# A two-layer transformer block with a hybrid mixer, then a second block with experts: another order of the last third of the mixer stage

## The chip, the cores and the metric

The kernel is one program on one core of a Trainium2 chip. The metric is the device time of one execution in microseconds; three executions of the kernel before gave 3403.52, 3405.39 and 3412.49 us, with the median at 3405.39 us.

## What is computed

The reference runs two layers of a first block (feed-forward, hybrid mixer, feed-forward, each added to the residual stream x) on 512 tokens of width 1024, and then a second block that the change does not touch. The change is in the hybrid mixer, which the kernel runs twice. The reference, cut to it:

```python
def hybrid_mixer(h, layer_idx, w_in, w_out, ...):
    proj = h @ w_in
    mq, mk, mv, mo, mi, mf, z, xbc, dt_raw, dq, dk, dv = jnp.split(proj, split_idx, axis=-1)
    ...
    hm = mlstm_chunkwise(...)                                   # 4 heads of 64
    y_mlstm = jax.nn.sigmoid(mo) * rms_norm(hm, mlstm_norm_w)
    ...
    y = (ssd_chunked(xs, dt, A, Bm, Cm) + D_skip * xs) * jax.nn.silu(z)
    y_ssm = rms_norm(y.reshape(..., SSM_GROUPS, -1), ssm_norm_w)  # 2 groups of 256
    dq, dk = rms_norm(dq, q_norm_w), rms_norm(dk, k_norm_w)
    o = diff_attention(dq, dk, dv, rel_bias, lam)               # 4 heads, causal, blocks of 128 queries
    y_diff = rms_norm(o, subln_w) * (1.0 - lam_init)
    return jnp.concatenate([y_mlstm, y_ssm, y_diff], axis=-1) @ w_out

def probs(qi, ki):                                              # inside a block of 128 queries
    logits = einsum(qi, ki) * scale + bias
    return softmax(where(mask, logits, -inf))
a = probs(q1, k1) - lam * probs(q2, k2)
out = einsum(a, v)
```

## The kernel before

The program is a list of stages. In each stage every engine walks the same list of steps, which `steps()` writes out by hand, and does its own part of each step; counting semaphores order the engines among each other, and each engine's own queue is strictly in the order of the steps. So the order in which `Mixer.steps()` yields decides what stands behind what on each engine.

**Items and sums.** The weights of the projections come as items, two halves of a block of 256 output columns. Items 0 to 17 of a mixer belong to earlier work. Items 18 and 19 give the attention's values (`dv`), 20 to 23 the gate z of the SSM, 24 and 25 the gate `mo` of the mLSTM; items 26 to 33 are the output projection. Every matrix product is made as three matmuls of a high and a low part (`mm3`). For a token item, `tok_pe` makes two tiles of 128 tokens of 24 matmuls each (128x256): 48 matmuls on TensorE, which then ticks `("sum", i)`. An item of the output projection is 24 matmuls of 128x512 (`fm_pe`), over eight 128-wide chunks of y in the order 2, 3, 4, 5 (SSM), 0, 1 (mLSTM), 6, 7 (attention).

**Splitting.** Before item i, `ahead(i)` yields `split` of item i+2: ScalarE casts the weights to the high part (`split_act`, line 387), GpSimd subtracts it to get the low part (`split_lo`, a line 167 operation on POOL). There are three buffers in turn, so the cast waits until the sum that reads the buffer has ended: for an even item i that is sum i-1, for an odd item i it is sum i itself. A token sum with an even number needs the low part of the item after it.

**Attention tiles.** The differential attention has 16 tiles, four heads times four blocks of queries. Tile n has width w = 128, 256, 384 or 512 (n mod 4). The step `diff` n is a software pipeline. On TensorE (`diff_pe`): the product with the values of tile n-3 (128x64), the two logit products qk of tile n (32x128 by w, into banks 2 and 3), the transposes of tile n-2. On VectorE (`diff_dve`): for tile n-1 a reciprocal (line 1894), a small product, a scaling and the difference of the two softmaxes; for tile n the two biased logits L (line 177, out of PSUM), two maxima (line 1914) and their negation `neg`. On ScalarE (`diff_act`): two copies out of PSUM for tiles n-3 (line 1875) and n-2 (line 1880), and the two exponentials of tile n (line 182). So a tile goes round a loop of VectorE and ScalarE: reciprocal and difference of the tile before, L, maxima, `neg`, exponentials, next reciprocal.

**What stands around them.** `droot` and `dfin` finish the norm of the attention's q and k: a reciprocal on VectorE, a root on ScalarE, and then `dfin`, 64 matmuls of 32x128 and four products on VectorE. `mnorm` 0 to 8 is the mLSTM norm (0 to 3 squares on POOL, 4 a reduction on VectorE, then four scalings), `zgate` and `ssq` the gate and the sums of squares of the SSM output, `sroot` and `snorm` its norm, `dnorm` the norm of the attention's output, `mo` the mLSTM gate. `turn` c transposes chunk c of y (4 transposes on TensorE), ScalarE casts the high part (line 2048) and VectorE subtracts the low part; then chunk c is ready for the output sums.

**Order before.** Items 18 and 19; `mnorm` 0 to 4, `droot`, `dfin`; then for each of items 20 to 25 the whole sum and behind it three attention steps; then `sroot`, `snorm` 0, turns 2 and 3, the last attention step, `snorm` 1, turns 4 and 5, `mo`, turns 0 and 1, `dnorm` 5 to 8, turns 6 and 7, and the eight output sums.

## Time and profile before

| | |
|---|---|
| median of three executions | 3405.39 us (3403.52 to 3412.49) |
| the profiled execution | 3405.64 us |
| its span, first to last instruction | 3403.4 us |
| mean granted TensorE clock | 0.947 |
| TensorE matmul busy | 3124.8 us (92%) |
| VectorE / ScalarE / GpSimd busy | 1641.5 / 1040.0 / 237.3 us |
| HBM traffic | 129 GB/s over the span |

"Busy" is the union of an engine's instructions; the granted clock is a share of full speed, 1.0 or 0.5 at any moment, and a mean over a stretch otherwise. The profiled execution is 0.25 us above the median.

### The profile page before, as it was taken

Reading aid. Unit: us, or ns where it says so; the run is one execution under the profiler, and the core shown is the slowest. Engines: PE = TensorE matmul, PEld = TensorE weight load, DVE = VectorE, ACT = ScalarE, POOL = GpSimd, SP = SyncE. Lnnn points to the kernel's source line nnn. Section 1 sums busy time; section 2 is a strip of 40 time slices with the busy share of each in tenths; the row PEclk is TensorE's granted clock in tenths of the full one; section 3 lists DMA queues with packets and bytes.
Section 4 is the critical chain, followed back from the end, with each engine's and each line's share of the span. In section 5 each row is a group of like instructions: output and inputs, shape, how many; then the busy total and the mean of one; then the engine's idle time right before and its main releaser. Section 6 shows DMA issues by size and latency. Waiting matters only on the chain. (4 is left out here: it accounts for less than half of the span.)

```text
span 3403.4 us, 41878 instructions
## 1 busy us (share of the span) xinstructions
PE 3124.8 (92%) x17296; PEld 2377.4 (70%) x17296; DVE 1641.5 (48%) x3102; ACT 1040.0 (31%) x2121; POOL 237.3 (7%) x171
## 2 busy tenths in 40 slices
PE   8999989879999999999999769999898899787887
PEld 6777768757888878888788658888686888332333
DVE  5444474364555554555563555444643674311212
ACT  4222245243323243333344333222332553000002
POOL 0000032121000000000121220000000210000000
PEclk9999989779999999999998779999889899899999
DMA  5443421102223222212211102222212004899997
GB/s 191 179 163 147 150 73 50 38 25 75 99 87 115 84 93 86 70 69 81 87 62 38 38 25 87 93 102 90 78 62 75 2 2 174 328 421 421 421 421 308
DMA packets 66164, 443.36 MB, mean 130 GB/s; under 512 B 7476, under 2 KB 7732, under 8 KB 19640
## 3 DMA queue, kind: packets, MB, share of 16 engines
q1 hardware_dynamic: 61056, 423.65, 32.8%
q10 hardware_dynamic: 3224, 10.49, 0.8%
q0 software_dynamic: 1696, 6.55, 0.5%
q8 instruction: 137, 2.24, 0.3%
q14 instruction: 51, 0.42, 0.0%
HBM read 435.16 MB, written 5.51 MB: 129 GB/s over the span
## 5 line engine op out<-in xcount | busy, mean ns | idle before, releaser
L157 PE MATMUL ps<-b,b 128*128 128x512 f32 (+7 forms) x13982 | 2799.8, 394 | 175.8 <-DVE b L167 58.4
L157 PEld LDWEIGHTS ps<-b,b 128*128 128x128 f32 (+3 forms) x13982 | 2097.1, 184 | 846.2 <-issue 321.3
L167 DVE TENSOR_TENSOR b<-b,b 128x1024 fp32r<-128x1024 f32 (+9 forms) x734 | 598.5, 820 | 274.1 <-ACT b L387 162.4
L387 ACT CAST b<-b 128x1024 fp32r<-128x1024 f32 (+2 forms) x408 | 392.0, 962 | 442.7 <-PE ps L157 437.5
L167 DVE TENSOR_TENSOR b<-ps,b 128x64 f32<-128x64 f32 (+5 forms) x617 | 215.3, 363 | 329.4 <-PE ps L157 274.2
L157 PE MATMUL ps<-b 64*64 64x64 f32 (+10 forms) x2848 | 268.0, 283 | 43.8 <-ACT b L1880 26.2
L167 POOL TENSOR_TENSOR b<-b,b 128x1024 fp32r<-128x1024 f32 (+3 forms) x120 | 202.8, 1706 | 1377.6 <-ACT b L387 947.2
L157 PEld LDWEIGHTS ps<-b 64*64 64x64 f32 (+3 forms) x2848 | 224.4, 164 | 83.5 <-ACT b L1880 31.2
L177 DVE SCALAR_TENSOR_TENSOR b<-ps,b 128x512 f32<-128x512 f32 (+3 forms) x272 | 142.4, 545 | 236.3 <-PE ps L157 211.7
L183 ACT ACTIVATE b<-b 128x512 f32<-128x512 f32 (+8 forms) x294 | 156.1, 538 | 236.1 <-DVE b L177 192.7
L167 DVE TENSOR_TENSOR b<-b,ps 128x512 f32<-128x512 f32 (+1 forms) x106 | 71.8, 678 | 280.0 <-PE ps L157 271.6
L177 DVE SCALAR_TENSOR_TENSOR b<-ps,b,b 128x128 f32<-128x128 f32 (+3 forms) x172 | 89.2, 545 | 222.4 <-ACT b L183 126.6
L1453 ACT CAST b<-b 128x512 fp32r<-128x512 f32 x88 | 54.6, 621 | 409.8 <-DVE b L167 409.8
L177 DVE SCALAR_TENSOR_TENSOR b<-b,b,b 128x512 f32<-128x512 f32 (+3 forms) x204 | 155.9, 778 | 43.2 <-ACT b L183 38.8
L183 ACT ACTIVATE b<-ps 128x512 f32<-128x512 f32 (+5 forms) x114 | 48.4, 439 | 382.3 <-PE ps L157 381.1
L177 DVE SCALAR_TENSOR_TENSOR b<-b,b 128x512 f32<-128x512 f32 (+6 forms) x235 | 142.9, 622 | 40.7 <-ACT b L183 38.2
L183 ACT ACTIVATE b<-b,b 128x128 f32<-128x128 f32 (+2 forms) x240 | 102.0, 465 | 121.1 <-DVE b L167 106.7
L285 PE MATMUL ps<-b,b 128*128 128x128 f32 (+2 forms) x466 | 85.5, 326 | 51.4 <-DVE b L177 30.0
L285 PEld LDWEIGHTS ps<-b,b 128*128 128x128 f32 (+2 forms) x466 | 62.2, 165 | 88.5 <-DVE b L177 33.5
L183 ACT ACTIVATE b<-ps,b 128x128 f32<-128x128 f32 (+3 forms) x148 | 59.9, 442 | 132.6 <-PE ps L157 129.7
L1018 ACT COPY b<-ps 128x128 f32<-128x128 f32 x240 | 60.2, 269 | 79.1 <-PE ps L157 69.6
L1133 POOL MEMSET b<- 128x128 f32 x12 | 2.6, 265 | 1010.0 <-DVE b L2545 586.9
(99 smaller groups left out, 559.6 us busy)
## 6 DMA issues: line engine op xcount, KB each, us to landing
b<-in_eg SPq DMA_DIRECT2D x64, 1024.0 KB, 27.3
b<-in_eu SPq DMA_DIRECT2D x64, 1024.0 KB, 27.2
b<-in_ed SPq DMA_DIRECT2D x64, 1024.0 KB, 27.1
b<-in_wg SPq DMA_DIRECT2D x44, 1024.0 KB, 4.8
b<-in_wu SPq DMA_DIRECT2D x44, 1024.0 KB, 4.9
b<-in_win SPq DMA_DIRECT2D x40, 1024.0 KB, 4.8
b<-in_wd SPq DMA_DIRECT2D x48, 768.0 KB, 4.2
b<-in_wmod SPq DMA_DIRECT2D x24, 1024.0 KB, 5.3
```

The source lines that it names most:

```text
L157: return e.h.matmul(out, l, r, start=start, stop=stop)
L167: return e.h.tensor_tensor(out, a, b, op)
L177: return e.h.scalar_tensor_tensor(out, a, s, b, op0, op1)
L183: return e.h.activation(out, a, f, bias=bias, scale=scale)
L285: return e.h.transpose(out, i, self.K["ident"][0:n, 0:n])
L387: e.h.copy(hi, src).then_inc(*self.S.tick(("hi", i)))
L1018: e.h.copy(self.LB[q][:, 0:128], B[:, 0:128]).then_inc(*S.tick((s, j, "L", lev + 1)))
L1133: z = e.h.memset(t, 0.0)
L1453: e.h.copy(self.ahi[:, f - self.f0[grp], :], t).then_inc(*S.tick(("ahi", f)))
```

## The change

In `Mixer.steps()`:

- `droot` comes ahead of `mnorm` 0 to 4, the second root is a step of its own (`mroot`), and `dfin` stands behind the whole sum of item 20 instead of ahead of it, followed by attention steps 0 and 1.
- Items 21 to 25 are cut in two on TensorE: `suma` i makes the first token tile (24 matmuls), then comes one attention step, then `sum` i makes the second tile and ticks. Two attention steps follow for items 21 to 24, none for item 25.
- Attention steps 15 to 18 stand in the tail, with `sroot`, `snorm` 0, turns 2, 3 behind step 15, `snorm` 1, turns 4, 5 behind step 16, `mo`, two squares of `dnorm` and turns 0, 1 behind step 17.
- The first two output sums are begun early: `part` 0 (18 matmuls, chunks 2, 3, 4, 5, 0, 1) ahead of step 18, `part` 1 behind it. Their last six matmuls each wait for turns 6 and 7. The banks of the output sums go 4, 5, 6, 7 instead of 6, 7, 4, 5.

```diff
-        for t in (2 * half, 2 * half + 1):
+        for t in [2 * half + j for j in tiles]:
...
-        p.then_inc(*self.P.tick(("sum", i)))
+        if tiles[-1]:
+            p.then_inc(*self.P.tick(("sum", i)))
...
+    def out_pe(self, e, j, places):
+
+        i = self.np + j
+        hi, lo, _ = self.views(i)
+        e.wait_ge(self.lo.at(("lo", i)))
+        for n in places:
+            c = self.order[n]
+            e.wait_ge(self.V.at(("ylo", c)))
+            p = mm3(e, self.k.bank[self.bank(i)][:, :], (hi[:, c, :], lo[:, c, :]), self.op(c), n == 0, n == 7)
+        if places[-1] == 7:
+            p.then_inc(*self.P.tick(("sum", i)))
...
             yield from self.ahead(i)
+            if i > 20:
+                yield "suma", i
+                yield "diff", diff
+                diff += 1
             yield "sum", i
...
             if i == 19:
+                yield "droot", 0
                 for j in range(5):
                     yield "mnorm", j
-                yield "droot", 0
+                yield "mroot", 0
+            elif i == 20:
                 for j in (0, 2, 1, 3):
                     yield "dfin", j
-            if i >= 20:
-                for j in range(3):
+                yield "diff", 0
+                yield "diff", 1
+                diff = 2
+            elif i > 20:
+                n = 0 if i == 25 else 2
+                for j in range(n):
                     yield "diff", diff
                     diff += 1
-                    if j == 1 and i in (21, 22, 23, 24):
-                        yield "mnorm", i - 16
-                    if diff >= 16:
-                        yield "dnorm", diff - 16
+                if i < 25:
+                    yield "mnorm", i - 16
...
+        for n in range(diff, 19):
+            yield "diff", n
+            if n == 15:
+                yield "sroot", 0
+                yield "snorm", 0
+                yield "turn", 2
+                yield "turn", 3
+            elif n == 16:
+                yield "snorm", 1
+                yield "turn", 4
+                yield "turn", 5
+            elif n == 17:
+                yield "mo", 0
+                yield "dnorm", 0
+                yield "dnorm", 1
+                yield "turn", 0
+                yield "turn", 1
+                yield "part", 0
+            elif n == 18:
+                yield "part", 1
...
-            return (6, 7, 4, 5)[(i - self.np) % 4]
+            return 4 + (i - self.np) % 4
...
-                self.fm_pe(e, i, B[self.bank(i)], 512, self.op, lambda c: V.at(("ylo", c)), self.order)
+                self.out_pe(e, j, range(6, 8) if j < 2 else range(8))
```

On TensorE, around item 20 of the first mixer, the order changes like this (the 32x128 matmuls are `dfin`; 128x256 are those of a token sum; `b_126` 128x128, 128x256 and 128x384 are the qk products of tiles 0, 1 and 2; the row of line 285 is a transpose):

```order
@@ -2282,5 +2282,4 @@
 L157 MATMUL ps<-b_129,b_134 128x256
 L157 MATMUL ps<-b_54,b_72 128x4 x4
-L157 MATMUL ps<-b_54,b_117 32x128 x64
 L157 MATMUL ps<-b_127,b_133 128x256
 L157 MATMUL ps<-b_130,b_133 128x256
@@ -2331,8 +2330,7 @@
 L157 MATMUL ps<-b_131,b_133 128x256
 L157 MATMUL ps<-b_128,b_134 128x256
+L157 MATMUL ps<-b_54,b_117 32x128 x64
 L157 MATMUL ps<-b_126 128x128 x2
 L157 MATMUL ps<-b_126 128x256 x2
-L157 MATMUL ps<-b_126 128x384 x2
-L285 MATMUL ps<-b_54,b_126 128x128
```

The 64 matmuls of `dfin` move behind the 48 of sum 20, and the products of tile 2 move away from those of tile 1, behind the first half of sum 21.

On ScalarE, from the exponentials of tile 1 to those of tile 2 (line 182 with widths 256 and 384; line 387 is the cast of a weight split, here of item 23; line 1880, in the changed kernel 1912, is the copy of tile 0's transposes; the ACTIVATE of line 183 puts sum 21 away), before:

```order
L182 ACTIVATE b_126,b_121<-b_126,b_121 128x256
L1880 COPY b_126<-ps 128x128 [waits mix_sums]
L182 ACTIVATE b_126,b_122<-b_126,b_122 128x384 [waits mix_vecs]
L182 ACTIVATE b_126,b_122<-b_126,b_122 128x384
L387 CAST b_127<-b_51 128x1024 [waits mix_sums]
L183 ACTIVATE b_126<-ps 128x2x256
```

and now:

```order
L182 ACTIVATE b_126,b_121<-b_126,b_121 128x256
L387 CAST b_127<-b_51 128x1024 [waits mix_sums]
L1912 COPY b_126<-ps 128x128
L182 ACTIVATE b_126,b_122<-b_126,b_122 128x384 [waits mix_vecs]
L182 ACTIVATE b_126,b_122<-b_126,b_122 128x384
L183 ACTIVATE b_126<-ps 128x2x256
```

The cast, which waits for the whole of sum 21, now stands ahead of the exponentials of tile 2; the same holds at items 23 and 25 for tiles 8 and 14.

On TensorE in the tail (128x64 are products with the values; line 285 are transposes, those of the attention tiles and of the turns):

```order
 L157 MATMUL ps<-b_126 128x512 x2
-L285 MATMUL ps<-b_54,b_126 128x128 x2
+L285 MATMUL ps<-b_54,b_126 128x128 x10
 L157 MATMUL ps<-b_126 128x64 x2
-L285 MATMUL ps<-b_54,b_126 128x128 x3
+L285 MATMUL ps<-b_54,b_126 128x128 x11
 L157 MATMUL ps<-b_126 128x64 x3
 L285 MATMUL ps<-b_54,b_126 128x128 x12
-L157 MATMUL ps<-b_126 128x64 x4
-L285 MATMUL ps<-b_54,b_126 128x128 x24
 L157 MATMUL ps<-b_135,b_127 128x512
```

Eight transposes of turns follow each of tiles 15, 16 and 17's steps, and the product with the values of tile 15 (the x4) leaves its place ahead of the output sums; it now stands between the two part sums.

## Rows read from the trace of the kernel before

**Rows 1.** Windows, both mixers: stretch, us, busy PE PEld DVE ACT POOL, clock, DMA, GB/s

```profile
626.70:821.70 195.00, 150.73 (x901) 126.05 (x902) 101.49 (x223) 69.60 (x169) 42.02 (x25) 0.79 0.11 38
1869.20:2064.20 195.00, 149.56 (x901) 125.27 (x902) 99.95 (x224) 69.69 (x169) 42.01 (x25) 0.79 0.11 38
```

**Rows 2.** Windows of the first mixer, piece by piece

```profile
643.14:649.50 6.36, 6.36 (x129) 5.75 (x129) 2.24 (x3) 0.99 (x2) 2.36 (x1) 0.57 0.01 3
649.50:655.20 5.70, 5.70 (x50) 5.64 (x48) 0.75 (x1) 0.00 (x0) 0.00 (x0) 1.00 0.02 4
750.00:775.60 25.60, 9.15 (x41) 8.17 (x41) 13.90 (x31) 7.09 (x19) 0.75 (x1) 0.50 0.00 0
```

**Rows 3.** Timeline around `dfin`: start, us, engine, instruction, idle before and its releaser

```profile
636.02 2.34 POOL L167 TENSOR_TENSOR b<-b,b 128x1024 fp32r<-128x1024 f32 x1 [13.62 <-ACT b L387]
640.67 1.22 DVE L2214 TENSOR_REDUCE b<-b 128x16 f32<-128x1024 f32 x1 [4.81 <-POOL b L167]
643.14 12.21 PE L157 MATMUL ps<-b,b 128*32 128x128 f32 x176 [7.50 <-ACT b L183]
```

**Rows 4.** Timeline, reciprocals of tiles 0 to 4, 6, 7, 15

```profile
658.21 0.17 DVE L1894 RECIPROCAL b<-b 128x2 f32<-128x2 f32 x1 [1.33 <-ACT b L182]
661.95 0.17 DVE L1894 RECIPROCAL b<-b 128x2 f32<-128x2 f32 x1 [1.16 <-ACT b L182]
666.65 0.17 DVE L1894 RECIPROCAL b<-b 128x2 f32<-128x2 f32 x1 [1.37 <-ACT b L182]
674.97 0.17 DVE L1894 RECIPROCAL b<-b 128x2 f32<-128x2 f32 x1 [1.59 <-ACT b L182]
678.57 0.17 DVE L1894 RECIPROCAL b<-b 128x2 f32<-128x2 f32 x1 [0.17 <-ACT b L182]
691.82 0.17 DVE L1894 RECIPROCAL b<-b 128x2 f32<-128x2 f32 x1 [1.37 <-ACT b L182]
697.46 0.17 DVE L1894 RECIPROCAL b<-b 128x2 f32<-128x2 f32 x1 [0.80 <-ACT b L182]
746.28 0.17 DVE L1894 RECIPROCAL b<-b 128x2 f32<-128x2 f32 x1 [1.59 <-ACT b L182]
```

**Rows 5.** Timeline, logits and `neg` of tile 2, one undisturbed turn

```profile
663.14 1.01 DVE L177 SCALAR_TENSOR_TENSOR b<-ps,b 128x384 f32<-128x384 f32 x2
665.11 0.17 DVE L172 TENSOR_SCALAR b<-b 128x2 f32<-128x2 f32 x1
```

**Rows 6.** Timeline, token sum 21, and logits that waited for sums 21 and 22

```profile
661.70 7.75 PE L157 MATMUL ps<-b,b 128*128 128x256 f32 x48
670.70 1.29 DVE L177 SCALAR_TENSOR_TENSOR b<-ps,b 128x512 f32<-128x512 f32 x2 [2.58 <-PE ps L157]
688.30 1.02 DVE L177 SCALAR_TENSOR_TENSOR b<-ps,b 128x384 f32<-128x384 f32 x2 [4.72 <-PE ps L157]
```

**Rows 7.** Timeline, `zgate` and splits on POOL, and VectorE beside them

```profile
702.36 2.90 POOL L167 TENSOR_TENSOR b<-b 128x512 f32<-128x512 f32 x2 [16.52 <-DVE b L177]
702.80 0.16 DVE L1894 RECIPROCAL b<-b 128x2 f32<-128x2 f32 x1
705.38 2.33 DVE L177 SCALAR_TENSOR_TENSOR b<-b,b 128x128 f32<-128x128 f32 x1
710.38 0.17 DVE L1894 RECIPROCAL b<-b 128x2 f32<-128x2 f32 x1 [1.16 <-ACT b L182]
723.48 2.20 DVE L172 TENSOR_SCALAR b<-b 128x2 f32<-128x2 f32 x1
744.53 0.17 DVE L172 TENSOR_SCALAR b<-b 128x2 f32<-128x2 f32 x1
```

**Rows 8.** Timeline of the tail

```profile
755.03 1.97 PE L285 MATMUL ps<-b,b 128*128 128x128 f32 x8 [5.50 <-DVE b L177]
775.58 52.56 PE L157 MATMUL ps<-b,b 128*128 128x512 f32 x224
782.70 0.69 DVE L167 TENSOR_TENSOR b<-ps,b 128x512 f32<-128x512 f32 x1 [4.76 <-PE ps L157]
```

More of the change, by code:

```diff
@@ L411, in fm_pe, with tok_pe @@
         t.then_inc(*self.P.tick(("sum", i)))
-    def tok_pe(self, e, i, bank, src, ready):
+    def tok_pe(self, e, i, bank, src, ready, tiles=(0, 1)):
         half = self.items[i].half
@@ L1607, in steps @@
             if i == 19:
+                yield "droot", 0
                 for j in range(5):
                     yield "mnorm", j
-                yield "droot", 0
+                yield "mroot", 0
+            elif i == 20:
                 for j in (0, 2, 1, 3):
                     yield "dfin", j
-            if i >= 20:
-                for j in range(3):
+                yield "diff", 0
[4 more added lines that the diff above has]
+                for j in range(n):
                     yield "diff", diff
                     diff += 1
-                    if j == 1 and i in (21, 22, 23, 24):
-                        yield "mnorm", i - 16
-                    if diff >= 16:
-                        yield "dnorm", diff - 16
+                if i < 25:
+                    yield "mnorm", i - 16
             if i in (22, 24):
                 yield "zgate", i // 2 - 11
-            if i in (23, 25):
+            elif i in (23, 25):
                 yield "ssq", i // 2 - 11
-        yield "sroot", 0
-        yield "snorm", 0
-        yield "turn", 2
-        yield "turn", 3
-        yield "diff", diff
-        yield "snorm", 1
+        for n in range(diff, 19):
[18 more added lines that the diff above has]
+                yield "part", 1
+        yield "dnorm", 2
         yield "dnorm", 3
-        yield "turn", 4
-        yield "turn", 5
         yield "dnorm", 4
-        yield "mo", 0
-        yield "turn", 0
-        yield "turn", 1
         for t in range(4):
@@ L1689, in pe @@
                 self.norm_pe(e, B[7], 512, self.before.V.at(("add", 7)))
-            elif name == "sum" and i < self.np:
+            elif name in ("sum", "suma") and i < self.np:
                 it = self.items[i]
@@ L1700, in pe @@
                         e.wait_ge(V.at(("Sd", 3, it.half)))
-                    self.tok_pe(e, i, B[it.half], self.hp, lambda c: V.at(("h", c)))
+                    tiles = (0, 1) if i <= 20 else (0,) if name == "suma" else (1,)
+                    self.tok_pe(e, i, B[it.half], self.hp, lambda c: V.at(("h", c)), tiles)
+            elif name == "part":
+                self.out_pe(e, i, range(6))
             elif name == "sum":
@@ L1706, in pe @@
                 elif j >= 2:
-                    e.wait_ge(V.at(("ylo", j + 2)))
-                else:
                     e.wait_ge(S.at(("yd", 15)), S.at(("AT", 15)))
-                self.fm_pe(e, i, B[self.bank(i)], 512, self.op, lambda c: V.at(("ylo", c)), self.order)
+                self.out_pe(e, j, range(6, 8) if j < 2 else range(8))
             elif name == "small":
@@ L2000, in act @@
                 act(e, self.dcol, self.dcol, ACT.Sqrt).then_inc(*S.tick("droot"))
+            elif name == "mroot":
                 e.wait_ge(V.at("mrec"))
```

## The prediction, made before the changed kernel ran

> **What bounds the kernel now.** I read the page first: TensorE matmuls are busy 92% of the span at a mean granted clock of 0.947, so only stretches in which TensorE waits or runs at half clock can give time. Then the windows over the changed stretch. From 626.7 us on, 195 us long, TensorE is busy 150.7 us at clock 0.79, and 1242.5 us later the second mixer does the same to 1.2 us of busy time [rows 1]. So whatever I work out for the first mixer counts twice. The timeline shows three different limits inside it.
>
> At the start, TensorE idles 7.50 us ahead of `dfin` [rows 3], because VectorE first waits 4.81 us for POOL's squares and only behind the mLSTM reduction makes the reciprocal that the root needs. `dfin` then takes 6.36 us in a stretch of clock 0.57 [rows 2].
>
> In the tile run, the loop of VectorE and ScalarE sets the pace, not TensorE. The time from one reciprocal to the next, where nothing disturbs it, is 3.60 us for a tile of width 128 (678.57 less 674.97), 3.74 us for 256, 4.70 us for 384, and 5.64 us for 512 (697.46 less 691.82) [rows 4]. From tile 0's reciprocal to tile 15's that makes 4 x 17.68 less the first 3.60 = 67.1 us. Measured: 746.28 less 658.21 = 88.1 us. So 21 us are disturbances, and only these can be won or moved.
>
> At the end, from the `neg` of tile 15 (744.70, the end of its row [rows 7]) to the first output sum (775.58 [rows 8]), everything is a chain of roots, scalings, transposes, casts and subtractions. TensorE is busy 9.15 of 25.6 us there, at clock 0.50 [rows 2].
>
> **Term 1, the start.** Now sum 20 fills the wait. It can't start when TensorE runs dry (635.64): it needs the low part of item 21, whose cast waits for sum 19, and POOL finishes that at 636.02 + 2.34 = 638.36 [rows 3]. TensorE has then paused 2.7 us, so I give the sum the 7.7 us that a token sum behind light work took (7.75 [rows 6]) and not the 5.7 us of the one at clock 1.00 [rows 2]: it ends at 646.0. The root is long ready. `dfin` at full clock shows in no row. Its bounds are 3.0 us, four products of 0.75 us on VectorE, and the 6.36 us it took now [rows 2]. I take 4.0, since a whole sum stands right ahead of it. The qk product of tile 0 starts at 650.0 instead of 655.28 (the end of the old row, 643.14 + 12.21, less a little [rows 3]). **Gain 5.3 us**, bounds 2.9 and 6.3. The reduction of `mnorm` 4 moves behind the reciprocal and is hidden under sum 20. If it were uncovered it would cost its 1.22 us.
>
> **Term 2, the tile run.** The disturbances now are: waits for whole sums at tile 3 (8.32 us from reciprocal to reciprocal where 5.64 is natural, 2.7 us [rows 4]) and at tile 6 (its logits waited 4.72 us for TensorE, and the turn is 4.8 us late [rows 6]); two `zgate` steps, in whose place the loop stands 1.7 us for the tanh and the product, each; and VectorE operations that lie beside a POOL operation and end only when it ends. Behind `zgate` three do, the last of them the difference of tile 8, which takes 2.33 us and ends with POOL's split; so the turn from tile 8's reciprocal to tile 9's is 7.58 us where 3.74 is natural [rows 7], 3.85 us, twice. At tile 12 a `neg` of 0.17 us takes 2.20 us, and the whole turn comes 2.3 us late [rows 7]. Sum: 2.7 + 4.8 + 3.4 + 7.7 + 2.3 = 20.9 us, which is the 21 found above.
>
> In the new order TensorE's extra work comes in pieces of 24 matmuls: 2.9 us at full clock (half of the 5.7 at clock 1.00 [rows 2]), and some 4.4 us when the piece starts at half clock. TensorE has made the qk product of a tile about one turn ahead of its use. The first half therefore lies under a turn of 3.6 to 5.6 us and costs nothing. Its cover is that turn: without it, it would cost the whole 2.9 to 4.4 us. The second half lies between the products of tile n and n+1. It ends about 3.5 us after the logits of tile n start, and the product for the next tile 1.2 us later, while VectorE wants it 3.7 to 5.6 us after: nothing, at worst 1 us.
>
> But at items 21, 23 and 25 the cast of the next split now stands ahead of the exponentials of tile n on ScalarE and waits for the second half. Queued behind it are two copies and the exponentials; VectorE waits for those. From the start of the logits the half ends at 3.5 us, the cast of 1.04 us at 4.5, the copies at 5.2. The `neg` of a tile of width 384 is ready after 2.14 us [rows 5], of width 128 after some 1.1. So each could cost 3 to 4 us, 10.3 us in all. I don't take that much, because TensorE runs ahead of VectorE by whatever VectorE loses elsewhere. I walked through the three places with the natural turns. At tile 2 TensorE has nothing older to do and starts the half before the logits: 1.0 us. Tile 8 follows a `zgate`, which delays VectorE by 3.8 us and TensorE not at all: 0. At tile 14, behind the other `zgate` but with a longer run of TensorE: 1.3 us. Together 2.3 us.
>
> `zgate` now has no split right behind it on POOL: 1.9 us for tanh and product plus 1.9 us for its two own POOL operations, against 5.6 before, twice: 7.6 us. The other splits fall on other VectorE operations of tiles 2, 5, 8, 11 and 14, at 0.4 to 1.1 us each by where they come in the turn: 3.9 us. Sum after: 2.3 + 7.6 + 3.9 = 13.8 us. **Gain 20.9 less 13.8 = 7.1 us.** Bounds: 13 us, if only the `zgate` waits stay; and -1 us, if the casts cost their 10.3.
>
> **Term 3, the tail.** I count from the end of tile 15's `neg`, called N (744.70). Before: first output sum at N + 30.9. The output sums go at 52.56 us for 224 matmuls [rows 8], 0.235 us each, so 192 of them take 45.1 us, and the half clock at their start adds 1.4 (first result added at 782.70, 7.1 us in, where 24 x 0.235 is 5.6): done at N + 77.3. Now: exponentials 1.6, table load and root 1.5, N + 3.1; `snorm` 0 1.7, turns 2 and 3 up to the last subtraction 3.4 (the turn begins at 755.03 now [rows 8]), N + 8.3; the difference of tile 15 1.6, `snorm` 1 1.7, turns 3.4, `mo` 1.4, N + 16.4; turns 0 and 1 occupy TensorE to N + 18.4. Then `part` 0 can run: 18 x 0.235 = 4.2 us and 1.4 for the half clock, N + 24.1; the product with the values of tile 15 to N + 25.1; `part` 1 to N + 29.3. That product was early before and now stands behind `part` 0, and the attention norm waits for it: copy, square, reduction, root, four scalings of 3.3 us end at N + 31.5, turns 6 and 7 with cast and subtraction at N + 34.9. TensorE has paused and starts slowly again: 156 matmuls are left, 36.7 us and 1.5: done at N + 73.1. **Gain 4.2 us**, bounds 1 (one more slow start and a late split of item 28) and 7 (no pause).
>
> **Sum.** 5.3 + 7.1 + 4.2 = 16.6 us per mixer, 33.2 us for both: 3405.6 less 33.2 = **3372.4 us**. The median of the runs before is 0.2 us off the profiled execution, which is nothing here.
>
> **Rivals.** (a) The disturbances only move: the loop is at its pace, POOL collides with VectorE as often as before, and the tile run gives nothing. For it speaks that 10 of the 21 us have nothing to do with sums. Left are 2 x (5.3 + 4.2) = 19 us: 3386.6 us. (b) The attention norm behind `part` 0 ends last and eats the tail's gain: 2 x (5.3 + 7.1) = 24.8, 3380.8 us. (c) The casts cost their full price, and terms 1 and 3 come near their lower bounds: 2 x (2.9 - 1 + 2) = 8 us, 3398 us, no change that can be told. (d) Slower: the cut sums keep TensorE slow. The row that speaks for it: sum 21, behind light work, took 7.75 us where sum 20 at clock 1.00 took 5.7 [rows 2, 6], and the tail ran at 0.50. If every half ran at half clock, it would take 5.9 us. Then the cast at tiles 2, 8 and 14 ends 7.9 us after the logits, which delays the exponentials by 5.8, 6.9 and 5.8 us, and the second halves of 22 and 24 come 3.7 and 1.8 us late: 24 us in place of 2.3. The tile run loses 14.6, the tail keeps 1.5: 5.3 - 14.6 + 1.5 = -7.8 us per mixer, 3421 us. It turns slower than before from a half of some 4.9 us on. Against it: `dfin`, 64 small matmuls in a row, was enough for the sum behind it to run at clock 1.00 [rows 2], and a half is a denser piece than that.
>
> [...]
>
> **How the numbers follow.** A measurement of this kernel can tell about 0.3% from no change, 10 us. Chances: the forecast as summed 0.62, (a) 0.16, (b) 0.07, (c) 0.09, (d) 0.06. The first three are faster by more than 10 us: 0.85; same 0.09, slower 0.06. The range goes from 3355 (terms at 6.3, 12 and 7) to 3397, just short of (c).
>
> **What the changed profile would show.** TensorE's wait ahead of `dfin` gone, and about 2.7 us ahead of sum 20 in its place; tile 0's reciprocal near 653; tile 15's near 734 instead of 746.3; VectorE's waits for TensorE small, its waits for ScalarE at tiles 2 and 14 about 1 us longer; the first 128x512 matmul about 18 us behind tile 15's `neg`; the stretch from 626.7 near 178 us instead of 195. Wrong would be: halves of nearly 6 us, a granted clock under 0.79 over the stretch, or exponentials that wait 3 us or more behind a cast at each odd item.

## The result, and the profile of the changed kernel

The changed kernel took a median of 3378.4 us (3374.2 to 3387.0, four runs), the kernel before, on the same chip, 3404.5 us (3403.5 to 3412.5): a ratio of 0.9922, 95% interval 0.9897 to 0.9946. It is faster, by 26 us where 33.2 were forecast, and the time lies in the range. The profiled execution is the slowest of the four: 3387.0 us with a span of 3385.0, against 3405.6 and 3403.4. So there are only 18.4 us between the two traces, and the first question is where the other half of the forecast went.

From the page of the changed kernel, its first two parts:

```profile
span 3385.0 us, 41880 instructions
...
PE 3130.5 (92%) x17296; PEld 2380.4 (70%) x17296; DVE 1647.8 (49%) x3102; ACT 1039.3 (31%) x2121; POOL 237.4 (7%) x171
...
PEclk9999999779999999999998879999899898899999
```

It doesn't show anything of the question: busy share and clock are those of before. A cut at landmarks does. I take the cast of item 21's weights on ScalarE as the start of the changed stretch, the second `ACTIVATE` of the output sums' results as its end, and a copy of 128x384 out of PSUM on ScalarE, 126 us earlier, as the start of token sums 13 to 19, which no line of the change touches. The windows of the kernel before (stretch, us, busy PE PEld DVE ACT POOL, clock, DMA share, GB/s), sums 13 to 19 and then the changed stretch, for either mixer:

```profile
508.80:634.90 126.10, 124.57 (x752) 107.21 (x750) 44.45 (x107) 53.27 (x143) 23.72 (x10) 0.93 0.12 42
634.90:805.80 170.90, 126.67 (x764) 105.05 (x763) 92.83 (x210) 62.87 (x160) 39.61 (x24) 0.76 0.11 38
1751.40:1877.50 126.10, 124.58 (x751) 107.23 (x749) 44.34 (x106) 53.25 (x142) 23.72 (x10) 0.93 0.12 42
1877.50:2048.30 170.80, 125.46 (x765) 104.22 (x765) 91.25 (x210) 63.01 (x160) 39.60 (x24) 0.76 0.11 38
```

and of the changed kernel:

```profile
509.20:648.40 139.20, 137.67 (x751) 117.92 (x750) 44.47 (x106) 53.30 (x143) 23.70 (x10) 0.83 0.11 38
648.40:802.20 153.80, 120.84 (x764) 100.19 (x763) 93.86 (x210) 62.84 (x160) 39.74 (x24) 0.80 0.12 42
1746.50:1883.30 136.80, 135.27 (x751) 115.40 (x749) 44.52 (x107) 53.31 (x142) 23.76 (x10) 0.85 0.11 39
1883.30:2034.50 151.20, 118.64 (x763) 99.10 (x764) 95.63 (x210) 62.74 (x159) 39.75 (x24) 0.82 0.12 42
```

The changed stretch is 17.1 us shorter in the first mixer and 19.6 us in the second: 36.7 us, 3.5 more than forecast. But the same 751 matmuls of sums 13 to 19 took 13.1 and 10.7 us longer, with unchanged busy time on the other engines and a clock of 0.83 and 0.85 where it was 0.93. That is 23.8 us given back in code that the change leaves alone. The rest of the span is 5.5 us shorter, most of it in the last 885 us, where the DMA moves 250 GB/s; nothing was run to find out why. 36.7 - 23.8 + 5.5 = 18.4.

**The three terms**, in the first mixer first. The start:

```profile
651.99 12.22 PE L157 MATMUL ps<-b,b 128*128 128x256 f32 x176 [2.86 <-POOL b L167]
654.16 1.22 DVE L2247 TENSOR_REDUCE b<-b 128x16 f32<-128x1024 f32 x1 [4.22 <-POOL b L167]
666.96 0.17 DVE L1926 RECIPROCAL b<-b 128x2 f32<-128x2 f32 x1 [0.95 <-ACT b L182]
...
745.22 0.17 DVE L172 TENSOR_SCALAR b<-b 128x2 f32<-128x2 f32 x1
```

The 7.50 us of idle time ahead of `dfin` [rows 3] are gone. TensorE waits 2.86 us for item 21's split and then runs sum 20 and `dfin` in one go of 12.22 us. From the cast of item 21 (634.90, now 648.38) to tile 0's reciprocal (658.21 [rows 4], now 666.96) it was 23.3 us and is 18.6: gain 4.7, forecast 5.3. In the second mixer it is 17.3: gain 5.9.

From there to the end of tile 15's `neg`, 86.5 us [rows 4, 7] became 78.4 (745.39 less 666.96): gain 8.1, forecast 7.1. Of the ten halves in it, the first, second, third, seventh and tenth:

```profile
666.10 3.10 PE L157 MATMUL ps<-b,b 128*128 128x256 f32 x24
670.06 3.06 PE L157 MATMUL ps<-b,b 128*128 128x256 f32 x24
680.28 5.12 PE L157 MATMUL ps<-b,b 128*128 128x256 f32 x24
...
715.13 4.80 PE L157 MATMUL ps<-b,b 128*128 128x256 f32 x24
...
733.37 3.05 PE L157 MATMUL ps<-b,b 128*128 128x256 f32 x24
```

Eight of the ten take 3.05 to 3.10 us, full clock; two that start at half clock take 4.80 and 5.12. The tail:

```profile
763.66 5.85 PE L157 MATMUL ps<-b,b 128*128 128x512 f32 x18
...
770.15 4.42 PE L157 MATMUL ps<-b,b 128*128 128x512 f32 x18
776.64 1.67 PE L285 MATMUL ps<-b,b 128*128 128x128 f32 x8 [2.08 <-DVE b L167]
779.78 44.76 PE L157 MATMUL ps<-b,b 128*128 128x512 f32 x188 [1.47 <-DVE b L167]
825.00 5.36 PE L157 MATMUL ps<-b,b 128*128 128x128 f32 x26 [0.47 <-DVE b L463]
```

The first piece of an output sum stands 18.3 us behind `neg` (18 forecast) instead of 30.9 [rows 8], and the next stage's first matmul 79.6 us behind it instead of 83.9 (828.60 less 744.70): gain 4.3, forecast 4.2. Together 17.1, forecast 16.6. In the second mixer, with the same landmarks, the gains are 5.9, 7.1 and 6.5 us, 19.5 together. Of the 3.5 us by which the two mixers beat the forecast, 2.3 are the second mixer's tail.

**What lies inside the tile run** differs from the forecast. At tile 7 and 8, `zgate` on POOL, the split of item 25 and VectorE beside them:

```profile
701.85 1.03 ACT L387 CAST b<-b 128x1024 fp32r<-128x1024 f32 x1
702.23 2.87 POOL L167 TENSOR_TENSOR b<-b 128x512 f32<-128x512 f32 x2 [13.33 <-DVE b L177]
702.67 0.16 DVE L1926 RECIPROCAL b<-b 128x2 f32<-128x2 f32 x1
702.86 1.03 DVE L167 TENSOR_TENSOR b<-b,b 128x1 f32<-128x1 f32 x1
703.93 1.45 DVE L172 TENSOR_SCALAR b<-b,b 128x512 f32<-128x512 f32 x1
705.06 2.52 POOL L167 TENSOR_TENSOR b<-b,b 128x1024 fp32r<-128x1024 f32 x1
705.42 2.71 DVE L177 SCALAR_TENSOR_TENSOR b<-b,b 128x512 f32<-128x512 f32 x1
```

The split stands right behind `zgate` as before. Three VectorE operations end at 703.89, 705.38 and 708.13, just behind POOL's two products, which end at 703.87 and 705.09, and its split, which ends at 707.58. And at tile 2, where a cast stands ahead of the exponentials, it costs next to nothing: `neg` ends at 674.03, the exponential starts at 674.26.

```profile
673.15 1.04 ACT L387 CAST b<-b 128x1024 fp32r<-128x1024 f32 x1 [2.48 <-PE ps L157]
673.86 0.17 DVE L172 TENSOR_SCALAR b<-b 128x2 f32<-128x2 f32 x1
674.26 0.61 ACT L182 ACTIVATE b<-b,b 128x384 f32<-128x384 f32 x1
```

### The profile page after: what moved, and what is told of

Same layout as the page of the kernel before. It is cut to its first block and busy times, and to the rows that moved or that the text cites. A ratio compares the mean times of both kernels' runs of the same rounds, so it can differ in the third digit from the quotient of the medians.

```text
span 3385.0 us, 41880 instructions
## 1 busy us (share of the span) xinstructions
PE 3130.5 (92%) x17296; PEld 2380.4 (70%) x17296; DVE 1647.8 (49%) x3102; ACT 1039.3 (31%) x2121; POOL 237.4 (7%) x171
## 5 line engine op out<-in xcount | busy, mean ns | idle before, releaser
L177 DVE SCALAR_TENSOR_TENSOR b<-b,b,b 128x512 f32<-128x512 f32 (+3 forms) x204 | 158.4, 790 | 46.5 <-ACT b L183 42.0
L1454 ACT CAST b<-b 128x512 fp32r<-128x512 f32 x88 | 54.6, 621 | 411.3 <-DVE b L167 411.3
L1019 ACT COPY b<-ps 128x128 f32<-128x128 f32 x240 | 60.0, 268 | 79.2 <-PE ps L157 69.5
```

The lines of the kernel that those rows point to most:

```text
L177: return e.h.scalar_tensor_tensor(out, a, s, b, op0, op1)
L1019: e.h.copy(self.LB[q][:, 0:128], B[:, 0:128]).then_inc(*S.tick((s, j, "L", lev + 1)))
L1454: e.h.copy(self.ahi[:, f - self.f0[grp], :], t).then_inc(*S.tick(("ahi", f)))
```

## The experiments

Whole runs of this kernel spread by what sums 13 to 19 do (below), so I read each variant in its changed stretch, and give the ratio to the kernel before beside it. The stretch is cut once more: the start up to tile 0's reciprocal, the tile run up to tile 15's `neg`, and the tail. All in us, first mixer / second mixer:

| kernel | sums 13 to 19 | changed stretch | start | tile run | tail | ratio to before |
|---|---|---|---|---|---|---|
| before | 126.1 / 126.2 | 170.9 / 170.7 | 23.3 / 23.2 | 86.5 / 86.4 | 61.1 / 61.1 | 1 |
| changed | 139.2 / 136.8 | 153.8 / 151.2 | 18.6 / 17.3 | 78.4 / 79.3 | 56.8 / 54.6 | 0.9922 (0.9897 to 0.9946) |
| e1 changed, again | 125.9 / 126.1 | 154.3 / 151.8 | 17.6 / 17.6 | 79.3 / 79.2 | 57.4 / 55.0 | 0.9879 (0.9862 to 0.9897) |
| e2 whole sums | 126.0 / 136.8 | 158.4 / 158.0 | 17.5 / 17.3 | 84.1 / 84.0 | 56.8 / 56.7 | 0.9921 (0.9896 to 0.9946) |
| e3 old start | 126.0 / 126.1 | 158.2 / 158.2 | 23.2 / 23.2 | 78.2 / 78.2 | 56.8 / 56.8 | 0.9905 (0.9885 to 0.9925) |
| e4 old tail | 126.0 / 136.8 | 156.7 / 156.1 | 17.5 / 17.4 | 79.2 / 79.3 | 59.9 / 59.4 | 0.9920 (0.9901 to 0.9939) |
| e5 casts later | 133.6 / 133.6 | 146.3 / 146.4 | 17.4 / 17.4 | 76.2 / 76.2 | 52.7 / 52.7 | 0.9890 (0.9867 to 0.9914) |
| e6 both parts behind step 18 | 133.7 / 127.4 | 150.1 / 151.3 | 17.6 / 18.7 | 79.3 / 78.5 | 53.2 / 54.1 | 0.9880 (0.9851 to 0.9908) |
| e7 norm ahead of `part` | 136.8 / 126.1 | 149.2 / 149.5 | 17.3 / 17.6 | 79.3 / 79.3 | 52.6 / 52.6 | 0.9914 (0.9888 to 0.9940) |
| e8 gate on VectorE | 126.1 / 137.1 | 151.5 / 150.5 | 17.6 / 18.6 | 77.1 / 78.2 | 56.8 / 53.7 | 0.9887 (0.9864 to 0.9910) |
| e9 filled gap | 131.1 / 130.9 | 153.7 / 153.9 | 18.5 / 18.6 | 78.4 / 78.4 | 56.8 / 56.8 | 0.9886 (0.9863 to 0.9909) |
| e10 e5 and e7 | 136.7 / 133.8 | 146.2 / 146.2 | 17.4 / 17.4 | 76.2 / 76.2 | 52.6 / 52.6 | 0.9871 (0.9840 to 0.9903) |
| e11 e10 and e9 | 137.3 / 129.5 | 148.3 / 146.6 | 18.6 / 17.6 | 75.3 / 76.5 | 54.4 / 52.5 | 0.9879 (0.9853 to 0.9905) |
| e12 e10 and e8 | 137.1 / 136.9 | 144.9 / 146.1 | 18.6 / 17.3 | 74.0 / 74.3 | 52.4 / 54.5 | 0.9840 (0.9817 to 0.9863) |

The changed kernel's tail stands unaltered in six of these profiles (changed, e1, e2, e3, e8, e9), twelve mixers. Eight times it took 56.7 to 56.8 us, and once each 53.7, 54.6, 55.0 and 57.4. So a difference of 2 to 3 us in one mixer's tail can be the granted clock alone, and e1's two tails are no typical pair to compare with. The start and the tile run repeat to about 1 us.

**e1, the changed kernel once more.** No edit.

> The changed kernel once more, unaltered. In its first profile the changed stretch (from the cast of item 21's weights to the second result of the output sums) took 153.8 and 151.2 us in the two mixers, against 170.9 and 170.7 before, but the unchanged stretch ahead of it (items 13 to 19) took 139.2 and 136.8 us against 126.1 and 126.2, at half clock for 46.0 and 41.0 us against 17.1 and 17.1. Theory A (the slow clock there is chance of the single execution, and the change has nothing to do with it): in this profile items 13 to 19 come out at another time, somewhere from 126 to 140 us in each mixer independently, while the changed stretch stays within 3 us of 153.8 and 151.2. Theory B (the change makes the stretch ahead of it slower in some way): 137 to 139 us again in both.

Measured: a median of 3369.3 us against 3414.2 of the kernel before beside it (45 us apart, where the first comparison had 26), and a profiled execution of 3366.5. Its windows of sums 13 to 19 and of the changed stretch, first mixer:

```profile
510.70:636.60 125.90, 124.37 (x751) 107.08 (x749) 44.34 (x106) 53.26 (x142) 23.72 (x10) 0.93 0.12 43
636.60:790.90 154.30, 121.86 (x765) 101.74 (x764) 95.17 (x210) 62.78 (x159) 39.60 (x24) 0.80 0.12 42
```

The identical program ran sums 13 to 19 at clock 0.93 and in 126 us again. So the 24 us come and go in one and the same program (theory A); the changed stretch repeats to 0.6 us. Whether the change makes the long form more frequent is not shown: the kernel before has one profile, with the short form twice. Its eleven executions beside e1 went from 3401.6 to 3419.7 us, at mean clocks of 0.947 down to 0.943, so it has slower forms of its own.

**e2, whole token sums again**, the new start and tail kept.

```diff
-            if i > 20:
-                yield "suma", i
-                yield "diff", diff
-                diff += 1
             yield "sum", i
...
-                n = 0 if i == 25 else 2
+                n = 1 if i == 25 else 3
...
```

> The halves undone: sums 21 to 25 whole again, each ahead of its attention steps; start and tail as changed. Theory A (term 2 is right: waits for whole sums at tiles 3 and 6, and splits that collide behind zgate): the tile run is 5 to 8 us longer per mixer than in the changed kernel, the changed stretch 159 to 162 us, the whole 10 to 16 us slower. Rival (the disturbances only move, and the halves are worth nothing): changed stretch within 2 us of the changed kernel's, and the whole within 4 us.

Measured: the changed stretch is 4.1 and 6.2 us longer than in e1, a little less than theory A said. The tile run is 4.9 and 4.7 us longer; the rest is the tail's clock. The waits for whole sums are back: VectorE waits for TensorE 0.92 us ahead of tile 2's logits, 2.09 at tile 5 and 4.18 at tile 11, and the turns are 1.5, 2.2 and 4.3 us late (at tile 2 a `neg` beside a split adds 0.5). The logits of tile 5, 256 wide:

```profile
674.29 0.76 DVE L177 SCALAR_TENSOR_TENSOR b<-ps,b 128x256 f32<-128x256 f32 x2 [2.09 <-PE ps L157]
```

Cut sums are worth about 5 us a mixer.

**e3, the old start** (`mnorm` ahead of `droot`, `dfin` ahead of sum 20).

```diff
             if i == 19:
-                yield "droot", 0
                 for j in range(5):
                     yield "mnorm", j
+                yield "droot", 0
                 yield "mroot", 0
-            elif i == 20:
                 for j in (0, 2, 1, 3):
                     yield "dfin", j
+            elif i == 20:
                 yield "diff", 0
```

> The start undone: mnorm 4 ahead of droot and dfin ahead of sum 20, as before; halves and tail as changed. Theory A (term 1): 4.7 to 5.3 us per mixer come back, changed stretch 156 to 159 us, the whole 9 to 11 us slower. Rival (the wait for item 21's low part and a slower sum 20 give it back): within 2 us per mixer.

Measured: 3.9 and 6.4 us longer. From the cast to tile 0's reciprocal it is 23.2 us as in the kernel before, against 17.6 in e1. The start gives its own gain, 5.6 us in both mixers; the tile run behind it is 1.1 us shorter than in e1, and the tails differ by -0.6 and +1.8 us.

**e4, the old tail.** Attention steps 15 to 17 with `dnorm` 0 to 2 behind them, then `sroot`, `snorm` 0, turns 2 and 3, step 18, and so on; whole output sums, banks 6, 7, 4, 5.

```diff
-                self.out_pe(e, j, range(6, 8) if j < 2 else range(8))
+                self.out_pe(e, j, range(8))
...
-            return 4 + (i - self.np) % 4
+            return (6, 7, 4, 5)[(i - self.np) % 4]
```

> The tail undone: attention steps 15 to 17 behind item 25, turns and norms behind them in the old order, output sums whole in the old banks; start and halves as changed. Theory A (term 3): 4.2 us per mixer come back, changed stretch 156 to 158 us, the whole 8 to 9 us slower. Rival (the attention norm behind part 0 eats the gain): within 1 us per mixer.

Measured: 2.4 and 4.3 us longer, all of it in the tail; against the usual tail of 56.8 us it is 3.1 and 2.6. Of all kernels this one lets the tile run be read to its last tile, since no tail step stands in it. Over the natural turns of the prediction its 15 turns lose 0.2 us at tile 2, 0.7 at 3, 0.8 at 5, 1.7 and 3.8 at 7 and 8, 0.1 and 1.0 at 10 and 11, 1.7 and 3.6 at 13 and 14: 13.7 us (80.8 from reciprocal to reciprocal less 67.1), where 13.8 were forecast and the kernel before loses 20.9. A loss "at tile n" is one of the turn that ends with tile n's reciprocal.

**e5, the cast of an odd item behind the attention step.**

```diff
-            yield from self.ahead(i)
             if i > 20:
                 yield "suma", i
+                if i % 2 == 0:
+                    yield from self.ahead(i)
                 yield "diff", diff
                 diff += 1
+                if i % 2:
+                    yield from self.ahead(i)
+            else:
+                yield from self.ahead(i)
             yield "sum", i
```

> The changed kernel, but at items 21, 23 and 25 the split of the item after next stands behind the attention step instead of ahead of it, so that on ScalarE the exponentials of tiles 2, 8 and 14 no longer queue behind a cast that waits for the second half. The trace of the changed kernel shows these exponentials 0.2, 0.2 and 0.0 us behind their neg. Theory A (TensorE runs ahead and the casts cost nothing, less than the 2.3 us of the forecast): changed stretch within 1.5 us of 154.3 and 151.8 per mixer. Theory B (the forecast's 2.3 us or more are there in other places of the run): 2 to 4 us shorter per mixer.

Measured: 8.0 and 5.5 us shorter than in e1, more than either theory said; the tile run gives 3.0 of it in both mixers, as in theory B. What goes in the run is not the wait behind the cast, which was 0.2 us, but collisions: the split moves off `zgate`, and the turn of tile 8 loses 1.8 us in place of 3.8, that of tile 14 1.9 in place of 3.6 and that of tile 3 nothing in place of 0.7; 0.3, 0.8 and 0.6 us come back at tiles 6, 9 and 11. The tail gives the rest. From tile 15's reciprocal on it takes 44.3 us in place of 49.3 and 46.9, with the same pieces and the same two pauses of 2.08 and 1.47 us. What differs is the clock. The windows of the tail of the first mixer, e1 and then e5:

```profile
733.50:790.90 57.40, 44.56 (x181) 36.56 (x182) 28.44 (x50) 19.09 (x33) 14.19 (x8) 0.74 0.11 37
```

```profile
736.40:789.10 52.70, 39.43 (x182) 32.27 (x182) 28.86 (x49) 19.32 (x36) 15.02 (x9) 0.89 0.17 60
```

`part` 0 runs at full clock (4.44 us in place of 6.45 in e1 and 5.85 in the first profile). Both mixers of e5 show it, but no run shows why the clock rises earlier there.

**e6, both parts behind attention step 18.**

```diff
                 yield "turn", 1
-                yield "part", 0
             elif n == 18:
+                yield "part", 0
                 yield "part", 1
```

> The changed kernel, but the last attention step, the product with the values of tile 15, stands ahead of part 0 instead of between the two parts. Theory A (the attention norm waits for that product, and TensorE pauses some 2 us ahead of turns 6 and 7 and 1.5 us behind them for it): the norm starts 5.7 us earlier, the pause ahead of turns 6 and 7 is gone, the later one stays or grows: 2 to 3 us shorter per mixer. Rival (the pause is set by something else): within 1 us.

Measured: 4.2 and 0.5 us shorter. The two parts run as one piece of 36 matmuls in 9.92 us (10.82 in the second mixer), and TensorE no longer pauses ahead of turn 6; the 1.47 us ahead of the last pieces stay. Against the usual tail of 56.8 us the gain is 3.6 and 2.7, the 2 to 3 of theory A and a little more.

**e7, the attention norm begun ahead of `part` 0**: step 18 and `dnorm` 0 to 3 ahead of turns 0 and 1, `dnorm` 4 to 8 and turns 6 and 7 between the two parts.

```diff
...
+        yield "diff", 18
+        for j in range(4):
+            yield "dnorm", j
+        yield "turn", 0
+        yield "turn", 1
+        yield "part", 0
+        for j in range(4, 9):
+            yield "dnorm", j
         yield "turn", 6
         yield "turn", 7
+        yield "part", 1
```

> Beside the edit of the run before, the product of tile 15 stands ahead of turns 0 and 1, and turns 6 and 7 stand between part 0 and part 1, so that part 1 covers their cast and subtraction. Theory A: TensorE waits some 1.5 us ahead of turns 6 and 7 and not behind them, 4 to 5 us shorter per mixer than the changed kernel, the whole 8 to 10 us faster. Rival (a new wait for the norm's scalings of the same size takes the place): within 2 us per mixer.

Measured: 5.1 and 2.3 us shorter. Around the parts TensorE's timeline has one pause where it had two, and 206 matmuls in a row behind it:

```profile
770.65 1.10 PE L285 MATMUL ps<-b,b 128*128 128x128 f32 x8 [1.77 <-DVE b L167]
771.50 47.06 PE L157 MATMUL ps<-b,b 128*128 128x512 f32 x206
```

Against the usual tail of 56.8 us that is 4.2 us in both mixers, in theory A's range. So the attention norm behind `part` 0 did cost about as much as the change's tail wins (4.3 us). That cost was in the forecast's walk, and the 4.3 us are what is left over it.

**e8, the gate's product moved from POOL to VectorE.**

```diff
-            elif name == "zgate":
-                for m in range(2):
-                    ...
-                    e.wait_ge(V.at(("z", i, m)), V.at(("skip", 7)))
-                    tt(e, y, y, z, ALU.mult).then_inc(*G.tick(("gated", i, m)))
```

The same two products stand in VectorE's `zgate`, ticking VectorE.

> The changed kernel, but the SSM gate's product is made on VectorE instead of POOL (four products of about 0.7 us per mixer). In the changed kernel's trace the three VectorE operations behind the first zgate take 1.03, 1.45 and 2.71 us where 0.16, 0.48 and 0.75 are natural (3.8 us lost), behind the second 1.06, 1.33 and 0.48 (1.9 us lost). Theory A (they are slow because POOL works beside them on SBUF): the losses behind zgate go except where a split still falls there (some 2 us), 2.8 us of products come, so the changed stretch is 0 to 2 us shorter per mixer, and the small product beside no POOL operation takes 0.16 us again. Rival (they are slow for another reason, such as waiting for ScalarE): the small product stays at 1 us and the stretch grows by the 2.8 us.

Measured: 2.8 and 1.4 us shorter; the tile run gives 2.1 and 1.1. VectorE pays 1.2 us for each pair of products (tile 7 loses 2.9 us in place of 1.7), and the second place loses 0.1 us behind it in place of 3.6 (0.9 in the second mixer). At the first, item 25's split still falls on VectorE, and it shows the effect with no other POOL work about. In the first mixer it meets the product of 128x1, which takes 2.26 us and ends 0.02 us behind the split, and tile 8 loses 2.1 us:

```profile
691.38 2.34 POOL L167 TENSOR_TENSOR b<-b,b 128x1024 fp32r<-128x1024 f32 x1 [14.56 <-ACT b L387]
691.48 2.26 DVE L167 TENSOR_TENSOR b<-b,b 128x1 f32<-128x1 f32 x1
693.78 0.49 DVE L172 TENSOR_SCALAR b<-b,b 128x512 f32<-128x512 f32 x1
```

In the second mixer it meets the pair of gate products, which take 3.43 us in place of 1.28; tile 7 loses 5.1 us there, and tile 8, with its product at 0.16 us, nothing:

```profile
1924.93 3.43 DVE L167 TENSOR_TENSOR b<-b 128x512 f32<-128x512 f32 x2
1925.22 2.60 POOL L167 TENSOR_TENSOR b<-b,b 128x1024 fp32r<-128x1024 f32 x1 [14.04 <-ACT b L387]
```

So the rival, that these operations are slow for another reason, falls.

**e9, dense matmuls into the gap near 564 us.** Two steps of six 128x512 matmuls each are put between the light pieces of the SSM behind sum 13, into a bank whose next sum overwrites them. They add work whose result nothing reads.

```diff
-           13: (("B", 5), ("A", 7), ("B", 6), ("B", 7))}
+           13: (("B", 5), ("A", 7), ("F", 0), ("B", 6), ("F", 1), ("B", 7))}
```

> The changed kernel with twelve more 128x512 matmuls per mixer whose result nobody reads, six ahead of and six behind the SSM products of head 6, in item 13's step, where TensorE has light work and waits 0.7 and 0.6 us. Over the profiles so far the unchanged items 13 to 19 took 126.0 to 127.4 us in nine cases of eighteen or so and 133.6 to 139.2 us in the others, in each mixer by itself; in the slow cases the clock first falls at some 564 us, in that light work. Theory A (that fall is what starts the slow pattern): no fall there any more, items 13 to 19 take 126 to 129 us in both mixers, and the times of the six executions lie within 6 us of each other, where the changed kernel's went over 11 us. Theory B (the pattern starts for other reasons): still one of the two in some mixers, plus 1 to 3 us for the matmuls, and the same spread.

In executions with the long form of sums 13 to 19 the clock falls first at 565 us and five times in all, in the short ones only at about 600 and 615. What this does to the same group of matmuls shows first in e1 and then in the first profile of the changed kernel (TensorE timeline):

```profile
589.11 7.68 PE L157 MATMUL ps<-b,b 128*128 128x512 f32 x34
```

```profile
596.20 9.16 PE L157 MATMUL ps<-b,b 128*128 128x512 f32 x34
```

Measured in e9:

```profile
509.70:640.70 131.00, 130.16 (x763) 112.14 (x762) 44.33 (x106) 53.18 (x142) 23.73 (x10) 0.91 0.12 41
```

The fall near 564 is gone, but the clock falls at 578 instead. The twelve matmuls themselves take some 2.8 us at full clock (an estimate, 12 x 0.235 us from the output sums), so 131 us is the short form and 2 us more, in both mixers, and six executions lie within 6.3 us of each other. That is near theory A without meeting its 126 to 129 us; e11 decides.

**e10, e5 and e7 together.**

> The split behind the attention step at items 21, 23 and 25, and the tail of the run with turns 6 and 7 between the part sums, together. If they add: tile run 2.8 us and tail 2.4 to 4.8 us shorter per mixer than the changed kernel, changed stretch 144 to 148 us, the whole 10 to 14 us faster at the same mode of items 13 to 19. If the two exclude each other: 146 us or more.

Measured: 146.2 us in both mixers, the same as e5 alone; the two exclude each other. From tile 15's reciprocal on, e5 and e10 take 44.3 and 44.2 us. They get there by different ways: e5's tail has both pauses and 11.9 us of half clock, e10's has another order and 15.3 us of it. Its times spread from 3353.6 to 3378.6.

**e11, e10 with the filled gap of e9** (the same unread matmuls).

> The two edits of the run before and the twelve matmuls without a reader. By theory A of the filling matmuls: changed stretch 144 to 148 us and items 13 to 19 at 126 to 129 us in both mixers, so a median of 3352 to 3360 us with a spread under 8 us. By theory B: no better than without them, 3360 to 3370 us.

Measured: sums 13 to 19 took 137.3 and 129.5 us, and the six executions spread over 15.5 us. A filled gap doesn't keep the short form: theory A of e9 falls, and what starts the long form stays open.

**e12, e10 with the gate on VectorE (e8).**

> The two edits and the SSM gate's product on VectorE. With the product on POOL the split no longer stands behind zgate once its cast is late, so little is left to win: tile run within 1.5 us per mixer of the run with the two edits alone. If the collisions with the gate's own product on POOL cost their 1.9 us twice and the products hide behind the exponentials: 2 to 4 us shorter per mixer.

Measured: a ratio of 0.9840 (0.9817 to 0.9863), a median of 3356.7 us: it beats the kernel before clearly, and the changed kernel (0.9922 and, again, 0.9879) at the edge of e1's interval. Its profiled execution is the slowest of seven, 3378.4 us with the long form in both mixers; the others lie at 3354.5 to 3359.9, and less the 22 us of the long form the profiled one would lie there too. Its tile run is 2.2 and 1.9 us shorter than e10's, so the second theory holds, at the lower end of its 2 to 4 us. Its changed stretch, and VectorE in the turn of the first gate:

```profile
646.50:791.40 144.90, 117.64 (x763) 98.67 (x764) 90.46 (x214) 62.15 (x159) 34.59 (x20) 0.84 0.13 44
```

```profile
699.42 1.29 DVE L167 TENSOR_TENSOR b<-b 128x512 f32<-128x512 f32 x2
...
700.82 0.16 DVE L167 TENSOR_TENSOR b<-b,b 128x1 f32<-128x1 f32 x1
701.01 0.48 DVE L172 TENSOR_SCALAR b<-b,b 128x512 f32<-128x512 f32 x1
701.53 0.75 DVE L177 SCALAR_TENSOR_TENSOR b<-b,b 128x512 f32<-128x512 f32 x1
```

Neither `zgate` nor a split lies on POOL here. The product, the scaling and the difference that took 1.03, 1.45 and 2.71 us beside POOL take 0.16, 0.48 and 0.75 us: 3.8 us, which is the whole loss of tile 8 in the changed kernel. That turn, from tile 7's reciprocal to tile 8's, takes 3.59 us here, the natural length, and 7.39 in the changed kernel.

## Why the prediction was right, and where it was not

**The sum** was right for the work it spoke of: 33.2 us forecast, 36.7 measured in the changed stretches of the first profile and 35.5 in e1's. The step that failed is an unwritten one, a term put at nothing without a reason: that what the change leaves alone takes as long as before. In the profiled execution sums 13 to 19 gave back 23.8 us, in e1 nothing. The median, 26 us below before, mixes both, and so does every median in the table; in e1 it was 45 us below. The range of 42 us happened to be wide enough for it; it had been made for other doubts. That the first median fell within 6 us of the forecast is in part luck.

**Term 1** (5.3 forecast): 4.7 and 5.9 us, and 5.6 to 5.7 in e1. The wait ahead of sum 20 is 2.86 us, forecast 2.7. The sum and `dfin` take 12.22 us at first and 11.13 in e2, forecast 7.7 + 4.0 = 11.7. The reduction of `mnorm` 4 is hidden, as said. e3 shows the gain to hang on these steps alone.

**Term 2** (7.1 forecast): 8.1 and 7.1 us, and 7.2 in e4 (20.9 less 13.7), where no tail step disturbs it. The sum of disturbances is right and three of its members are not. "`zgate` now has no split right behind it on POOL" had no reason beside it and was wrong. The cast for the split of item 25 waits for the whole of sum 23, which ended at 701.80; it was done at 702.88, with `zgate` on POOL until 705.09, and the split followed it. The two places cost 1.7 + 3.8 and 1.7 + 3.6 = 10.8 us, forecast 7.6. The casts cost 0.2 us, forecast 2.3; that TensorE was further ahead than my walk had it fits the rows, but no run set it apart. The other splits cost 2.6 us, forecast 3.9. +3.2, -2.1 and -1.3 cancel, by luck.

**Term 3** (4.2 forecast): 4.3 us in the first mixer and 6.5 in the second. The pauses are the same in both; in the second the clock had risen by `part` 0 (4.43 us in place of 5.85). The forecast gave each slow start 1.4 to 1.5 us and could not know in which mixers the clock would spare it. The pauses that the rival (b) lived on are 2.08 and 1.47 us, near what the walk had. Undoing the tail costs 2.4 and 4.3 us.

The three parts undone one at a time give back 5, 5 and 3 us a mixer (means), 13.6 in all, where the change wins 17.7. They are not independent, and most of the difference lies in the tile run: e2 gives back 4.8 of its 7.2 us, and in e3 it is 1.1 us shorter.

**The rivals.** (a), the disturbances only move, falls: 7.2 us of them are gone. It held for the gate and its split, which moved nowhere. (b) falls: the tail's 4.3 us are there with the norm behind `part` 0. The cost behind it is real, though: e6 and e7 take 2.7 to 4.2 us off the usual tail. (c), casts at full price, falls at tile 2's 0.2 us. (d), halves at half clock, falls: eight of ten take 3.05 to 3.10 us, against the 5.9 that it needs and the 4.9 from which it turns. The clock of the stretch rose from 0.76 to 0.80 and 0.82. The Trainium skill, "TensorE: Matmul & The Clock Gate", section "Loop structure matters more than you think", has matmuls back to back as its good case and a long wait ahead of every matmul as its bad one. These rows lie between the two: pieces of 24 matmuls with light products and short waits between them, eight of ten at full clock.

**The signs.** Tile 0's reciprocal came at 667.0, not near 653: late by the 13.1 us that sums 13 to 19 lost. Counted from item 21's cast, it was forecast at 18.1 us and came at 18.6. Tile 15's reciprocal was forecast near 734 and came at 753.5. Besides the 13.1 us that is a wrong sign: in the new order the first tail steps stand ahead of it on VectorE, and its turn takes 12.2 us where e4, without them, has 5.64. It's the `neg` of tile 15 that can be compared, and it came at 745.2. The signs should have been given as distances from a landmark in the same stretch.

## What to carry to other kernels

Compare two traces by stretches between landmarks that both kernels have, and look first at the stretches that the change doesn't touch: what moves there is the noise of the comparison, and here it was as large as two thirds of the effect. Where VectorE's loop sets the pace, look for what runs on GpSimd beside it; a pair of products of 1.2 us on VectorE was cheaper than the same pair on GpSimd, beside which VectorE's own operations stood. A long sum can be cut into short dense pieces between light products, if each is covered by a turn of the loop that waits for it.

## What was not expected of the hardware

- **Some VectorE operations with all operands in SBUF make no way beside a running GpSimd operation.** A product of 128x1 took 1.03 us beside POOL and 0.16 alone, a difference of 128x512 2.71 and 0.75 us, a `neg` 2.20 [rows 7] and 0.17. They end a little behind POOL's operation: the product of 128x1, 0.16 us long alone, 0.02 us behind it (e8), the difference of 128x512, 0.75 us alone, 0.55 us (708.13 less 707.58). So most of the work comes after POOL has ended. Reciprocals (0.16 us), maxima, though their operands lie in SBUF, and logits that are read from PSUM weren't held: 1.00 and 1.02 us for two of width 384 beside the split of 737.58, as long as alone, where the `neg` behind them took 0.40.

```profile
737.58 2.35 POOL L167 TENSOR_TENSOR b<-b,b 128x1024 fp32r<-128x1024 f32 x1 [0.58 <-ACT b L387]
737.59 1.02 DVE L177 SCALAR_TENSOR_TENSOR b<-ps,b 128x384 f32<-128x384 f32 x2
738.52 1.00 DVE L1946 TENSOR_REDUCE b<-b 128x1 f32<-128x384 f32 x2
739.56 0.40 DVE L172 TENSOR_SCALAR b<-b 128x2 f32<-128x2 f32 x1
```

  The Trainium skill, "Trainium Architecture — The Big Picture", section "What this means for kernel authors", calls the port pair that VectorE and GpSimd share an exclusive lock and not a split of bandwidth. The held rows agree, and e12, with POOL's product gone and the split elsewhere, shows the price: 3.8 us in one turn.
- **The same 751 matmuls in the same program take 126 or 137 to 139 us,** each mixer for itself (e2, e4, e7 and e8 have both forms in one execution), at a mean granted clock of 0.93 or 0.83 to 0.85. Forms of 127.4 (e6) and 133.6 to 133.8 us (e5, e6, e10) occur too; those were seen with other orders behind them only. Once the clock falls early in the stretch, it falls again in the later light pieces too (at 565, 579, 593, 606 and 623 us in the first profile, at 599 and 613 in e1). What sets it off was looked for in one gap (e9, e11) and not found there.
